# Warming products on written ones, the constants on ScalarE's DMA queue, and u's fourth block copied before the first sines

## The chip, the cores and the metric

One core of one Trainium2 chip runs the whole program. The metric is the device time of one execution in microseconds (us). Of the kernel before, three runs are shown, with their median. A profile of one further execution gives the span that the trace covers.

## What is computed

Two blocks of a model work one after the other on 256 tokens of width 1024, all in float32. The change touches only the first microseconds of the first block:

```python
h = rms_norm(x, norm_w)                  # x: 256 x 1024
proj = h @ w_in                          # u_s is the first 1024 of its columns
# s5_branch(u_s): a complex diagonal recurrence over the 256 tokens,
# per group: ab = exp(lam * dt), bb = f(lam, dt) * b, y = Re(C h) + d * u
...
x = x + m @ w_o
# second block: two gated mixers, then 32 experts, two for each token
hid = silu(xb @ w1[e]) * (xb @ w3[e])
out = out.at[tok].add((hid @ w2[e]) * w)
```

## The kernel before

The program is written by hand for each engine: five instruction streams (SyncE, ScalarE, VectorE, GpSimd, TensorE), joined by semaphores. The order inside each stream is the order of the Python code. Weights stream from memory through the ring, a few slots in one large tile `mem`, each DMA waiting until the products that read its slot are done.

What the start does, by engine:

- SyncE's queue issues the DMAs: the first part of the constants (`con`, 202.5 KB: the unit matrix, ones, the parameters of the recurrence), then x turned (`x_turned`, a view of `xn`) in two halves, between them the weights of u's first two blocks, then the rest of u's weights, `ssm_b`, `ssm_c`, the other constants, and the weight units one after the other.
- TensorE first runs six products of the unit matrix with `con` into bank 7, whose results nobody reads. Then it projects u in eight blocks (`project_u`), of 16 records each in the trace (every product of 256 columns in float32 is two records). Blocks 0 and 1 are made from the input times its gains (`raw`), blocks 2 to 7 from the normed input `hT`. Two PSUM banks are used in turn (`pj`), so block j waits until block j - 2 has been copied out. Between block 0 and block 1 stands the sum of squares, between block 3 and block 4 the inputs of the first two pairs of the scan. The 26 dense projections follow, and before them TensorE waits until blocks 6 and 7 of u are copied out.
- ScalarE squares the input, copies u's blocks 2 to 7 out of PSUM (`take_u`), and makes decay factors, sines and cosines for each of 16 pairs (`trig(pr)`: seven activations and at times a table load). `trig(pr)` waits for the angles of pair pr (`phase_ready`, VectorE's `angle_sums`).
- VectorE multiplies the gains onto x, adds the squares, works out the recurrence's parameters in small instructions (`decay_factors`), scales blocks 0 and 1 of u and makes `hT`. Then come the tables of angles, the angles of pair 0, those of the rotary embedding (`rope_angles`), and for each pair the rotation and two scans.
- GpSimd waits for `ssm_c`, scales it in six instructions of 1024 columns (L589 to L591), and then finishes the states of each pair (L601 to L606).

`banks[7]` is next used by the experts, and `Hr_` by GpSimd's first pair.

Of the kernel before, what the change touches and what calls it, by code (L numbers as in the profile page):

```python
# [48 lines left out]
NCONST1 = CONST_AT["none"][0]  # L49
# [44 lines left out]
def mark(ins, sig):  # L94
    sig.made += 1
    ins.then_inc(sig.sem, 1)
    return sig.made


def link(eng, ins, sig):  # L100

    eng.wait_ge(sig.sem, mark(ins, sig))
# [149 lines left out]
def build(nc, A, out):  # L252
    stack = ExitStack()
    with stack:
        def sb(name, shape, dt=F32):
            return stack.enter_context(nc.sbuf_tensor(name, shape, dt))

        def sem(name):
            return stack.enter_context(nc.semaphore(name))
# [7 lines left out]
        con = sb("con", [P, NCONST])  # L267
        small = sb("small", [P, 972])
        psum = stack.enter_context(nc.psum_tensor("psum", [P, 8, 512], F32))
        banks = [psum[:, i, :] for i in range(8)]  # L270

        def C(name):
            a, w = CONST_AT[name]
            return con[:, a:a + w]

        ident = C("ident")
# [3 lines left out]
        def carve(start, sizes):  # L280

            got, at = [], start
            for n in sizes:
                got.append(area[:, at:at + n])
                at += n
            assert at <= 22528, at
            return got

        def bc(ap, shape):
            return ap.to_broadcast(shape)  # L290
# [9 lines left out]
        def load_unit(sp, n):  # L300
            s = n % SLOTS_BLOCKS
            if n >= SLOTS_BLOCKS:

                pj.to_read(sp, last_fill[FRONT[n - SLOTS_BLOCKS][0]])
            sp.dma_start(ring[:, s, :], A["front"][n]).then_inc(slot_loaded[s], 16)
# [83 lines left out]
        def load_sixth(sp, side):  # L389
# [14 lines left out]
        uT_, BTr_, BTi_, CTr_, CTi_, fa_, fb_, Hr_, Hi_, ptmp2, qT_, kT_, v_ = carve(  # L404
            0, [2048, 1024, 1024, 1024, 1024, 512, 512, 1024, 1024, 512, 3072, 3072, 3072])
# [65 lines left out]
        for name, s in ([(f"u{n}", PJ_U + 4 * n + 3) for n in range(2)]  # L471
# [8 lines left out]
        con_in, con2_in, misc_in, bt_in, ct_in, xre_in = (sem(s) for s in (  # L480
            "con_in", "con2_in", "misc_in", "bt_in", "ct_in", "xre_in"))
# [3 lines left out]
        act1, dve1, pool1 = Signal(sem("act_step1")), Signal(sem("dve_step1")), Signal(sem("pool_step1"))  # L485
# [60 lines left out]
            return range(TP_ATT + 2 * a, TP_ATT + 2 * a + 2)  # L546

        def sync_of_first_layer(sp):
            sp.dma_start(con[:, 0:NCONST1], A["constants"][:, 0:NCONST1]).then_inc(con_in, 16)
            for n in range(2):  # L550
                sp.dma_start(x_turned[:, 4 * n:4 * n + 4, :], A["xT"][:, 4 * n:4 * n + 4, :]).then_inc(xT_in[n], 16)
                sp.dma_start(ring[:, 0, 1024 * n:1024 * n + 1024], A["front"][0, :, 1024 * n:1024 * n + 1024]).then_inc(u_block_in[n], 16)
            sp.dma_start(ring[:, 0, 2048:4096], A["front"][0, :, 2048:4096]).then_inc(slot_loaded[0], 16)
            for n, dst in enumerate((BTr_, BTi_)):
                sp.dma_start(dst, A["ssm_b"][n]).then_inc(bt_in, 16)
            load_unit(sp, 1)
            for n in range(2):
                sp.dma_start(c_raw[n], A["ssm_c"][n]).then_inc(ct_in, 16)
            sp.dma_start(con[:, NCONST1:], A["constants"][:, NCONST1:]).then_inc(con2_in, 16)
            for n in range(2, 2 + len(DENSE) + 2):  # L560
                load_unit(sp, n)

            sp.wait_ge(qk_ready.sem, 6)
            for s in range(2):
                tq.after_read(sp, 10 + s)
            sp.dma_start(xres[:, :, :], A["x"][0].rearrange("(i p) n -> p i n", p=P)).then_inc(xre_in, 16)
            sp.wait_ge(y_free.sem, 8)

            def load(dst, src, **kw):
                sp.dma_start(dst, src, **kw).then_inc(par2_in, 16)  # L570

            for r in range(2):
                load(lb2[:, r], A["hg_lb_2"][r].rearrange("(k p) -> p k", p=P), allow_slow_non_contiguous=True)
            load(hgain, A["hg_out_norm_2"][0].partition_broadcast(P))
            load(dgain[:, 0], A["da_q_norm_2"][0].partition_broadcast(P))
            load(dgain[:, 1], A["da_k_norm_2"][0].partition_broadcast(P))
            load(ogain, A["da_out_norm_2"][0].partition_broadcast(P))
            load(lamv, A["da_lambda_2"][0].partition_broadcast(P))
            for n in range(2 + len(DENSE) + 2, n_units1 + SLOTS_BLOCKS):
                load_unit(sp, n)  # L580
# [31 lines left out]

        def scalar_of_first_layer(act):

            act.dma_start(posi[:, :], A["att_positions"]).then_inc(misc_in, 16)
            act.wait_ge(con_in, 16)
            act.activation(prm[:, DT, :], given[:, DT, :], ACT.Exp).then_inc(dt_ready, 1)
# [13 lines left out]
            def take_u(j):  # L631
                pj.to_read(act, PJ_U + j)
                pj.emptied(act.activation(uT[:, j, :], pj.tile(j)[:, 0:256], ACT.Copy), PJ_U + j)  # L633

            def trig(pr):
                b = pr % 2
                act.wait_ge(phase_ready.sem, pr + 1)
                if pr >= 2:
                    act.wait_ge(state_ready.sem, pr - 1)
                act.activation(decay[:, b, :, 1:256], bc(mag_c[:, 2 * pr:2 * pr + 2].unsqueeze(2), [P, 2, 255]), ACT.Copy)  # L640
                mark(act.activation(sin_t[:, b], phase[:, b], ACT.Abs, bias=quarter_off), act1)
                link(act, act.activation(cos_t[:, b], phase[:, b], ACT.Abs), act1)
                mark(act.activation(sin_t[:, b], sin_t[:, b], ACT.Abs, bias=half_off), act1)
                link(act, act.activation(cos_t[:, b], cos_t[:, b], ACT.Abs, bias=half_off), act1)
                act.activation(sin_t[:, b], sin_t[:, b], ACT.Sin, scale=TURN, bias=halfpi_off)
                link(act, act.activation(cos_t[:, b], cos_t[:, b], ACT.Sin, scale=TURN, bias=halfpi_off), trig_ready)

            take_u(2)
            trig(0)
            for j in range(3, 6):  # L650
                take_u(j)
            trig(1)
            for j in range(6, 8):
# [110 lines left out]
            act.activation(rows2, banks[2][:, 0:256], ACT.Copy).then_inc(rows2_ready, 1)  # L764

        def tensor_of_first_layer(pe):
            pe.wait_ge(con_in, 16)
            for n in range(6):
                pe.matmul(banks[7][:, 0:256], ident, con[:, 0:256], start=True, stop=True)

            def sum_of_squares():
                pe.wait_ge(sq_added, 3)
# [183 lines left out]
            ins.then_inc(xT2_full, 1)  # L956

        def vector_of_first_layer(dve):
            dve.wait_ge(dt_ready, 1)
            R = lambda a: given[:, a, :] if a < DT else prm[:, a, :]  # L960
            mark(dve.tensor_tensor(R(LRDT), R(LR), R(DT), ALU.mult), dve1)
# [203 lines left out]
            for a in range(ATT_STEPS):  # L1165
# [9 lines left out]
                if a in (4, 5):  # L1175
                    n = a - 4
# [566 lines left out]
        @block.sync  # L1743
        def _(sp):
            sync_of_first_layer(sp)
            sp.wait_ge(m_done, 4)
            load_ahead(sp, 3)
# [40 lines left out]
        @block.scalar  # L1788
        def _(act):
            scalar_of_first_layer(act)  # L1790
            for h in range(4):
                pj.after_read(act, PJ_HF + h)
# [87 lines left out]
        @block.tensor  # L1880
        def _(pe):
            tensor_of_first_layer(pe)
            def turn(first, n_fills, blocks):

# [189 lines left out]
        @block.vector  # L2074
        def _(dve):
            vector_of_first_layer(dve)

            dve.wait_ge(rows2_ready, 1)
# [195 lines left out]
```

## Time and profile before

| | |
|---|---|
| three runs | 1087.08, 1085.91, 1088.96 us |
| median | 1087.08 us |
| span of the profiled execution | 1084.6 us |
| TensorE busy, products | 942.7 us |
| DMA, read and written | 292.91 MB |

The three runs are whole executions; the span is what the trace of a fourth one covers, 2.5 us less than the median of the three. For that fourth execution no time other than its span is listed. Times in the rows count from the span's start. A row of the timeline gives start, duration, engine, line, operation and operands, the count of instructions merged into it, and in brackets how long the engine had been idle and what ended that.

### The profile page before, as it was taken

How to read it: one execution, taken by the hardware profiler on the slowest of the kernel's cores; microseconds unless marked ns; L12 is line 12 of the kernel's file. 1: busy time of each engine (PE TensorE's matmuls, PEld its weight loads, DVE VectorE, ACT ScalarE, POOL GpSimd, SP SyncE). 2: the span in 40 equal slices, each digit the busy share in tenths (PEclk: the TensorE clock that was granted, in tenths of full speed). 3: DMA queues.
4: the chain of work that ended last, by engine and by line, in shares of the span. 5: the costliest groups of instructions: out<-in, count | busy, mean ns of one | idle time of the engine just before them, and what ended most of it. 6: DMA issues, size and time to landing. Idle time of an engine off the chain costs nothing.

```text
span 1084.6 us, 12689 instructions
## 1 busy us (share of the span) xinstructions
PE 942.7 (87%) x5090; PEld 555.3 (51%) x5090; DVE 419.4 (39%) x714; ACT 256.1 (24%) x627; POOL 155.4 (14%) x107
## 2 busy tenths in 40 slices
PE   8999999999999999999999998956766666665956
PEld 6655655668888857544788854423221313131412
DVE  7979898835622123253633314221111102020201
ACT  3595978424421012222222020000000000000000
POOL 1776777830000000000000000000000000000000
PEclk9999999999999999999999999998797969798788
DMA  9444243252244446543234699999999999999997
GB/s 366 184 156 149 85 156 136 105 189 88 79 155 155 155 156 257 192 148 134 79 146 154 264 424 387 428 424 426 425 430 424 430 426 430 428 427 428 427 429 318
DMA packets 29121, 292.91 MB, mean 270 GB/s; under 512 B 7568, under 2 KB 8592, under 8 KB 10640
## 3 DMA queue, kind: packets, MB, share of 16 engines
q1 hardware_dynamic: 28928, 292.24, 66.4%
q8 instruction: 33, 0.54, 0.2%
q14 instruction: 16, 0.13, 0.0%
q10 hardware_dynamic: 144, 0.00, 0.0%
HBM read 291.18 MB, written 1.05 MB: 269 GB/s over the span
## 4 chain that ended last, share of the span: by engine, by line
PE 58%; DMA 29%; DVE 5%; issue 3%; ACT 2%; POOL 2%; SPq 0%; DVEq 0%; POOLq 0%; ACTq 0%
DMA mem<-in_experts 29%; PE psum L338 15%; PE psum L345 8%; PE psum L329 7%; PE psum L317 6%; PE psum L322 5%; PE psum L1553 3%; PE psum L1533 2%; PE psum L1570 1%; PE psum L1580 1%; PE psum L1903 1%; PE psum L826 1%; PE psum L890 1%; PE psum L1585 1%; PE psum L878 1%
## 5 line engine op out<-in xcount | busy, mean ns | idle before, releaser
L1553 PE MATMUL psum<-mem 128*32 128x512 f32 x1016 | 144.1, 699 | 82.3 <-DMA mem<-in_experts 82.2
L329 PE MATMUL psum<-mem,hT 128*128 128x512 f32 x288 | 126.3, 595 | 0.5 <-ACT mem L633 0.5
L1553 PEld LDWEIGHTS psum<-mem 128*32 128x32 f32 x1016 | 30.9, 118 | 176.6 <-DMA mem<-in_experts 111.2
L338 PE MATMUL psum<-hT,mem 128*128 128x256 f32 x512 | 115.2, 381 | 0.0
L338 PEld LDWEIGHTS psum<-hT,mem 128*128 128x128 f32 x512 | 95.6, 190 | 15.9 <-issue 2.9
L329 PEld LDWEIGHTS psum<-mem,hT 128*128 128x128 f32 x288 | 55.7, 196 | 64.5 <-issue 63.5
L338 PE MATMUL psum<-mem 128*128 128x256 f32 x320 | 69.7, 379 | 0.0
L317 PE MATMUL psum<-mem,hT 128*128 128x512 f32 x160 | 69.2, 592 | 0.0
L1713 DVE SCALAR_TENSOR_TENSOR mem<-mem,psum 128x512 f32<-128x512 f32 x8 | 5.5, 687 | 155.1 <-ACT mem L1455 155.1
L338 PEld LDWEIGHTS psum<-mem 128*128 128x128 f32 x320 | 60.6, 190 | 8.1
L345 PE MATMUL psum<-hT,mem 128*128 128x256 f32 x256 | 57.6, 382 | 0.0
L1580 PE MATMUL psum<-mem 128*32 128x512 f32 x244 | 42.5, 809 | 16.4 <-DMA mem<-in_experts 12.0
L322 PE MATMUL psum<-mem 128*128 128x512 f32 x128 | 55.6, 592 | 0.0
L1453 ACT ACTIVATE mem<-psum 128x256 f32<-128x256 f32 x8 | 3.1, 383 | 212.4 <-PE psum L1561 212.4
L345 PEld LDWEIGHTS psum<-hT,mem 128*128 128x128 f32 x256 | 48.0, 190 | 7.0
L317 PEld LDWEIGHTS psum<-mem,hT 128*128 128x128 f32 x160 | 30.2, 190 | 36.9 <-issue 36.8
L1083 DVE TENSOR_TENSOR_SCAN mem<-mem 128x512 f32<-128x512 f32 x32 | 46.2, 1482 | 0.0
L1570 PE MATMUL psum<-mem 128*128 128x256 f32 (+1 forms) x96 | 36.6, 505 | 7.2 <-DVE mem L1718 7.2
L1722 DVE TENSOR_TENSOR xn<-xn,psum 128x256 f32<-128x256 f32 (+1 forms) x42 | 21.4, 510 | 53.5 <-PE psum L1570 53.3
L322 PEld LDWEIGHTS psum<-mem 128*128 128x128 f32 x128 | 24.2, 190 | 28.8 <-issue 28.7
L1533 PE MATMUL psum<-mem,xres 128*128 128x128 f32 x256 | 32.5, 288 | 7.0 <-issue 6.3
L1533 PEld LDWEIGHTS psum<-mem,xres 128*128 128x128 f32 x256 | 31.9, 204 | 8.6 <-issue 7.6
(368 smaller groups left out, 1208.2 us busy)
## 6 DMA issues: line engine op xcount, KB each, us to landing
mem<-in_experts SPq DMA_DIRECT2D x87, 2048.0 KB, 35.6
mem<-in_front SPq DMA_DIRECT2D x39, 2048.0 KB, 7.8
mem<-in_experts SPq DMA_DIRECT2D x15, 1024.0 KB, 34.4
con<-in_constants SPq DMA_DIRECT2D x1, 1035.0 KB, 18.2
xn<-in_xT SPq DMA_DIRECT2D x2, 512.0 KB, 5.4
mem<-in_front SPq DMA_DIRECT2D x2, 512.0 KB, 7.3
mem<-in_front SPq DMA_DIRECT2D x1, 1024.0 KB, 10.0
mem<-in_ssm_b SPq DMA_DIRECT2D x2, 512.0 KB, 11.1
```

What stands on the lines that cost most here:

```text
L317: ins = pe.matmul(dst, lhs[:, k, P * i:P * i + P], w[:, k, c0:c0 + 512], start=(k == 0), stop=(k == nk - 1))
L322: ins = pe.matmul(dst, lhs[:, k, P * i:P * i + P], w[:, k, c0:c0 + 512], start=(k == 0), stop=(k == lhs.shape[1] - 1))
L329: ins = pe.matmul(dst, tokens[:, k, i], w[:, k, :], start=(k == 0), stop=(k == KD - 1))
L338: ins = pe.matmul(dst[:, at:at + T], w[:, k, P * m:P * m + P], rhs[:, k, :], start=(k == 0), stop=(k == nk - 1))
L345: ins = pe.matmul(dst, w[:, k, P * m:P * m + P], rhs[:, k, :], start=(k == 0), stop=(k == nk - 1))
L826: ins = pe.matmul(banks[4 + 2 * (a % 2) + w][:, at:at + keys.stop - keys.start], qT[r, g, j, P * i:P * i + P], kT[r, g, j, keys], start=Tr ...
L1083: ins = dve.tensor_tensor_scan(out=dst[:, b], data0=decay_[:, 512 * b:512 * b + 512], data1=src, initial=0.0, op0=ALU.mult, op1=ALU.add)
L1533: ins = pe.matmul(bank[:, P * (k % 4):P * (k % 4) + P], xres[:, i, P * k:P * k + P], selx_[:, P * i:P * i + P], start=(i == 0), stop=(i == 1))
L1553: ins = pe.matmul(banks[m // 2 % 2][32 * q:32 * q + 32, :], xgT[:, k, 32 * q:32 * q + 32], w[q][:, FF * kk:FF * kk + FF], start=(k == 0), ...
L1570: pe.matmul(total(n), selT_[:, P * i:P * i + P], y_[:, at:at + width], start=True, stop=True).then_inc(combined, 1)
L1580: ins = pe.matmul(banks[2][r, :], hidT[:, k, r], w[q][:, 512 * kk:512 * kk + 512], start=(k == 0), stop=(k == 3), tile_position=(0, 32 * q))
L1722: dve.tensor_tensor(dst, x if isinstance(it, int) and it == 0 else dst, total(n), ALU.add).then_inc(added, 1)
```

## The change

Four edits. The constants' first DMA goes from SyncE's queue to the head of ScalarE's. TensorE's first products are five instead of six, on a stretch of `Hr_` that VectorE fills with 1.0 as its first instruction, and they wait for that instead of for the constants, for which TensorE now waits behind them. ScalarE copies u's block 3 before `trig(0)` instead of behind it.

```diff
         def sync_of_first_layer(sp):
-            sp.dma_start(con[:, 0:NCONST1], A["constants"][:, 0:NCONST1]).then_inc(con_in, 16)
             for n in range(2):
...
         def scalar_of_first_layer(act):
 
+            act.dma_start(con[:, 0:NCONST1], A["constants"][:, 0:NCONST1]).then_inc(con_in, 16)
             act.dma_start(posi[:, :], A["att_positions"]).then_inc(misc_in, 16)
             act.wait_ge(con_in, 16)
...
             take_u(2)
+            take_u(3)
             trig(0)
-            for j in range(3, 6):
+            for j in range(4, 6):
                 take_u(j)
             trig(1)
...
         def tensor_of_first_layer(pe):
+            pe.wait_ge(dve1.sem, 1)
+            for n in range(5):
+                pe.matmul(banks[7][:, 0:256], Hr_[:, 0:128], Hr_[:, 0:256], start=True, stop=True)
             pe.wait_ge(con_in, 16)
-            for n in range(6):
-                pe.matmul(banks[7][:, 0:256], ident, con[:, 0:256], start=True, stop=True)
...
         def vector_of_first_layer(dve):
+            mark(dve.memset(Hr_[:, 0:256], 1.0), dve1)
             dve.wait_ge(dt_ready, 1)
```

On ScalarE, from the activation of the norm (L629) to the start of pair 1's `trig`; L633 is `take_u`, L640 to L646 are one `trig`. Before:

```order
L629 ACTIVATE mem<-psum,con 128x256
L633 ACTIVATE mem<-psum 128x256
L640 ACTIVATE mem<-small 128x2x255
L641 ACTIVATE mem<-mem,con 128x512
L642 ACTIVATE mem<-mem 128x512
L643 ACTIVATE mem<-mem,con 128x512
L644 ACTIVATE mem<-mem,con 128x512
L645 ACT_TABLE_LOAD
L645 ACTIVATE mem<-mem,con 128x512
L646 ACTIVATE mem<-mem,con 128x512
L633 ACTIVATE mem<-psum 128x256 x3
L640 ACTIVATE mem<-small 128x2x255
```

And of the change, the same place:

```order
L629 ACTIVATE mem<-psum,con 128x256
L633 ACTIVATE mem<-psum 128x256 x2
L640 ACTIVATE mem<-small 128x2x255
L641 ACTIVATE mem<-mem,con 128x512
L642 ACTIVATE mem<-mem 128x512
L643 ACTIVATE mem<-mem,con 128x512
L644 ACTIVATE mem<-mem,con 128x512
L645 ACT_TABLE_LOAD
L645 ACTIVATE mem<-mem,con 128x512
L646 ACTIVATE mem<-mem,con 128x512
L633 ACTIVATE mem<-psum 128x256 x2
L640 ACTIVATE mem<-small 128x2x255
```

One copy has moved from behind pair 0's `trig` to before it; the copies of blocks 4 and 5 are still behind pair 0's, those of 6 and 7 behind pair 1's.

On SyncE's queue, the head of the program (xn is x turned, in_front the weights of u). Before:

```order
L549 DMA con<-in_constants 128x405
L551 DMA xn<-in_xT 128x1024
L552 DMA mem<-in_front 128x1024
L551 DMA xn<-in_xT 128x1024
L552 DMA mem<-in_front 128x1024
L553 DMA mem<-in_front 128x2048
L555 DMA mem<-in_ssm_b 128x1024 x2
L305 DMA mem<-in_front 128x4096
L558 DMA mem<-in_ssm_c 128x1024 x2
```

And of the change:

```order
L550 DMA xn<-in_xT 128x1024
L551 DMA mem<-in_front 128x1024
L550 DMA xn<-in_xT 128x1024
L551 DMA mem<-in_front 128x1024
L552 DMA mem<-in_front 128x2048
L554 DMA mem<-in_ssm_b 128x1024 x2
L305 DMA mem<-in_front 128x4096
L557 DMA mem<-in_ssm_c 128x1024 x2
```

Each DMA behind the constants has moved up by one place on SyncE's queue.

On TensorE, the first rows with their waits. Before:

```order
L769 MATMUL psum<-con 128x256 [waits con_in]
L769 MATMUL psum<-con 128x256 x5
L790 MATMUL psum<-xres,mem 128x256 [waits raw_ready,u_block0_in]
L790 MATMUL psum<-xres,mem 128x256 [waits raw_ready] x7
L774 MATMUL psum<-mem,con 128x256 [waits sq_added]
```

And of the change:

```order
L770 MATMUL psum<-mem 128x256 [waits dve_step1]
L770 MATMUL psum<-mem 128x256 x4
L792 MATMUL psum<-xres,mem 128x256 [waits raw_ready,u_block0_in,con_in]
L792 MATMUL psum<-xres,mem 128x256 [waits raw_ready] x7
L776 MATMUL psum<-mem,con 128x256 [waits sq_added]
```

The first product no longer waits for the constants, and block 0 of u does as well as for what it waited for.

## Rows read from the trace of the kernel before

**Rows 1.** Busy time of each engine, from the page.

```profile
PE 942.7 (87%) x5090; PEld 555.3 (51%) x5090; DVE 419.4 (39%) x714; ACT 256.1 (24%) x627; POOL 155.4 (14%) x107
```

**Rows 2.** Stages at the end: busy of PE, PEld, DVE, ACT, POOL; PEclk, DMA share, GB/s.

```profile
700.00:1085.00 385.00, 258.54 (x1830) 92.66 (x1822) 51.26 (x93) 15.65 (x35) 0.00 (x0) 0.84 0.99 419
```

**Rows 3.** The chain that ended last, 100 to 120 us.

```profile
101.16 2.14 POOL mem L606
...
112.08 0.68 ACT mem L710
```

**Rows 4.** TensorE's timeline, 43 to 320 us.

```profile
112.89 0.63 PE L865 MATMUL psum<-con,xres 128*128 128x128 f32 x4 [1.00 <-ACT mem L710]
```

**Rows 5.** GpSimd's and VectorE's timelines, 20 to 60 us.

```profile
23.19 2.27 POOL L589 TENSOR_TENSOR mem<-mem 128x1024 f32<-128x1024 f32 x1 [22.74 <-DMA mem<-in_ssm_c]
...
34.16 2.37 POOL L591 TENSOR_TENSOR mem<-mem 128x1024 f32<-128x1024 f32 x1
...
23.86 2.15 DVE L1053 TENSOR_TENSOR mem<-mem 128x512 f32<-128x512 f32 x1
...
34.35 2.66 DVE L1040 SCALAR_TENSOR_TENSOR small<-small 128x16 f32<-128x16 f32 x3
...
37.13 0.69 DVE L1053 TENSOR_TENSOR mem<-mem 128x512 f32<-128x512 f32 x1
37.73 0.68 DVE L1067 TENSOR_TENSOR mem<-mem,psum 128x512 f32<-128x512 f32 x1
```

**Rows 6.** All engines' timeline, 0 to 22 us.

```profile
0.74 0.40 SPq L549 DMA_DIRECT2D con<-in_constants  x1
...
1.19 0.42 SPq L551 DMA_DIRECT2D xn<-in_xT  x1
...
3.37 4.81 PE L769 MATMUL psum<-con 128*128 128x256 f32 x12 [3.37 <-DMA con<-in_constants]
...
8.20 3.72 PE L790 MATMUL psum<-xres,mem 128*128 128x256 f32 x16
...
9.41 1.14 DVE L989 TENSOR_SCALAR xres<-xn,con 128x256 f32<-128x256 f32 x4 [1.88 <-DMA xn<-in_xT]
...
15.82 1.74 DVE L1000 RECIPROCAL mem<-mem 128x256 f32<-128x256 f32 x1
```

**Rows 7.** Stages of the start, in the columns of rows 2.

```profile
1.50:2.50 1.00, 0.00 (x0) 0.00 (x0) 0.00 (x0) 0.97 (x1) 0.00 (x0) 1.00 0.64 122
...
4.00:6.50 2.50, 2.50 (x7) 1.95 (x6) 2.33 (x7) 1.97 (x5) 0.00 (x0) 1.00 0.82 220
...
12.00:32.00 20.00, 16.46 (x84) 13.39 (x84) 19.11 (x39) 6.80 (x12) 8.65 (x4) 1.00 1.02 428
```

**Rows 8.** The warming products by their line: ns min/median/max.

```profile
L769 PE MATMUL psum<-con x12: 379/631/792, 3.4 to 7.8; 128*128 128x256 f32 x12
```

**Rows 9.** TensorE's timeline, 17 to 45 us.

```profile
18.50 7.14 PE L790 MATMUL psum<-hT,mem 128*128 128x256 f32 x32 [1.37 <-DVE hT L1009]
...
26.65 3.72 PE L790 MATMUL psum<-hT,mem 128*128 128x256 f32 x16
32.38 10.60 PE L790 MATMUL psum<-hT,mem 128*128 128x256 f32 x48 [2.01 <-ACT mem L633]
43.50 1.96 PE L329 MATMUL psum<-mem,hT 128*128 128x512 f32 x4 [0.52 <-ACT mem L633]
```

**Rows 10.** ScalarE's timeline, 15 to 45 us.

```profile
26.04 0.63 ACT L640 ACTIVATE mem<-small 128x510 f32<-128x510 f32 x1 [3.44 <-DVE mem L1053]
...
31.85 0.66 ACT L633 ACTIVATE mem<-psum 128x256 f32<-128x256 f32 x2
36.10 0.38 ACT L633 ACTIVATE mem<-psum 128x256 f32<-128x256 f32 x1 [3.60 <-PE psum L790]
37.85 0.63 ACT L640 ACTIVATE mem<-small 128x510 f32<-128x510 f32 x1 [1.36 <-DVE mem L1053]
...
42.38 0.38 ACT L633 ACTIVATE mem<-psum 128x256 f32<-128x256 f32 x1
43.01 0.38 ACT L633 ACTIVATE mem<-psum 128x256 f32<-128x256 f32 x1 [0.25 <-PE psum L790]
```

## The prediction

> **What bounds the kernel now.** I read the page first: TensorE is busy for 942.7 us, 87% of the span [rows 1]. That share hides two regimes. In the last 385 us the DMA engines are busy for a share of 0.99 at 419 GB/s [rows 2], so the end waits for the experts' weights; those DMAs wait for ring slots that TensorE frees, so what TensorE gains or loses before about 600 us should move the end by as much. The question is what bounds TensorE in the first 113 us, where all four edits act.
>
> The chain that ended last answers it. At 112.08 us it is in a ScalarE copy (L710), before that in ScalarE's `trig`, and before that in GpSimd's L606 at 101.16 [rows 3]. TensorE's own timeline agrees: at 112.89 us it has been idle for 1.00 us, until that copy [rows 4], and from 43.50 to there it shows no idle time. So TensorE reaches 112 us with 1.00 us in hand, and time that it gains before only makes this wait longer. What counts is the chain through VectorE, GpSimd and ScalarE.
>
> I followed that chain back. VectorE's rotation of pair 0 (L1067) starts at 37.73, directly behind the angles of pair 1 (L1053, 37.13) [rows 5]. Ahead of that stand tiny instructions that take far longer than their size. The three L1040, on 16 columns, take 2.66 us together, and an L1053 at 23.86 takes 2.15 us where the one at 37.13 takes 0.69. All of it lies beside GpSimd's six products on `ssm_c`, from 23.19 to 34.16 + 2.37 = 36.53 us [rows 5]. The reader is to see that VectorE gets free only when GpSimd's last one ends, and that GpSimd's start is set by a landing: it waited 22.74 us for `ssm_c`. So the start of the path is the arrival of `ssm_c`, not the arrival of x, nor TensorE.
>
> Before 23 us VectorE is a chain of its own: it waits 1.88 us for the second half of x, starts on it at 9.41, and comes to the reciprocal at 15.82 [rows 6]; TensorE waits for it at 18.50. But its slack against GpSimd's hold begins at 23.86 - 23.19 = 0.67 us: up to that much earlier, its L1053 still falls into GpSimd's first product and ends with it.
>
> **Edit 1, the constants on the other queue.** SyncE's queue issues the constants at 0.74 and x's first half at 1.19 [rows 6], so each later DMA is issued 0.45 us earlier, `ssm_b`, the first whole unit and `ssm_c` among them. The bytes ahead of `ssm_c` stay the same, and from 12 to 32 us the engines are at a share of 1.02 [rows 7]: an earlier issue into a full pipe lands nothing earlier. What can be gained is the unused part at the start. From 1.50 to 2.50 the share is 0.64, so 1 x 0.36 = 0.36 us of all engines' time is free. From 4.00 to 6.50 it is 0.82 at only 220 GB/s, when more DMAs have been issued than can be in work, so issue isn't what is missing there [rows 7]. The bounds for `ssm_c` are 0 (all lost to the interleaving of two queues) and 0.45 us (the whole issue). I take 0.3, near the 0.36 that the row shows as free. For x's second half the same 0.3 holds; it is below 0.67, so it hides under GpSimd's hold. The Trainium skill, DMA: Bandwidth & Descriptors, section Issuing engines are not separate DMA queues, speaks against this edit: DMAs started by different engines run on the same 16 DMA engines and interleave, and only the sequencer's issue time is saved. By that rule the sum would be between the two bounds too, nearer to 0.
>
> The constants themselves may land later, as they now share the engines with x's first half. What waits for them is ScalarE's first exponential and VectorE's small chain, which comes to x's second half 1.88 us early [rows 6]: 1.88 us of cover, cost 0. ScalarE issues one more DMA, some 0.4 us by L549's row, before its first table load; the cover is the same. The position DMA, behind it, is read by VectorE only after 25 us. Cost 0.
>
> **Edit 2, the warming products.** They began at 3.37, when the constants landed, and took 4.81 us for 12 records, 0.40 us each; the next 16 took 3.72 us, 0.23 each [rows 6]. By duration they are 631 ns in the median and 379 at least [rows 8]: they ran at the lower of the two levels (1.2 GHz), and block 0 of u at the upper (2.4 GHz), though the clock column says 1.00 throughout. Now 10 records start behind a fill of 256 columns, at about 1.3 us (my estimate from the first activity at 1.19 us on ScalarE), and end at about 1.3 + 10 x 0.40 = 5.3. Then TensorE waits until the first weights of u, about 8.2 - 0.3 = 7.9 us. Whether block 0 then runs at the upper level is not to be read from any row. It decides little: all 16 records of block 0 at 0.40 us give 7.9 + 6.4 = 14.3, the sum of squares 4 x 0.40 later 15.9, and the norm on ScalarE some 0.5 us later, at 16.4, against VectorE's reciprocal at 15.82 [rows 6]. That is 0.6 us later at worst, within the slack that ends at GpSimd's second product at 25.4. I take 0. VectorE's fill of about 0.3 us lies in the time when it waits for the constants. Cost 0.
>
> **Edit 3, u's block 3 copied before the sines.** TensorE ends block 3 at 18.50 + 7.14 = 25.64, block 4 at 30.37, and then waits 2.01 us, till 32.38, for the copy of block 3, which stands behind `trig(0)` and comes at 31.85 [rows 9, 10]. Now the copy runs from about 25.7 to 26.1, the wait of 2.01 us goes, and `trig(0)`, behind it on ScalarE, starts at 26.1 instead of 26.04. Behind `trig(0)` VectorE waits at 37.73, and `trig(0)` ends at 31.85: 5.9 us of cover. So blocks 5 to 7 end 2.0 us earlier, at about 32.38 + 10.60 - 2.01 = 41.0. But what is late next? TensorE may go on only when blocks 6 and 7 are copied, and those copies stand behind `trig(1)`, which starts at 37.85 because it waited 1.36 us for VectorE's angles, and whose last sine is followed by the copies from 42.38 on [rows 10]. Both together take 0.66 us as the pair at 31.85 did, so TensorE starts at 42.38 + 0.66 + 0.11 = 43.15, where the 0.11 is the distance from the last copy's end (43.39) to 43.50 before. Of 2.01 us only 0.35 are left, and a wait of about 2.1 us stands at 41 us. And these 0.35 us come to 112.89, where TensorE waits anyway. The term is 0, with the bounds 0 and 2.0 (the wait gone for good).
>
> **The sum.** The chain at 37.13 moves with `ssm_c`: -0.3. Edits 2 and 3: 0. The span goes from 1084.6 to 1084.3. The runs' median stands 2.5 us above the span, so the time is 1087.08 - 0.3 = 1086.8 us.
>
> **Rivals.**
> 1. *Edit 1 does nothing*: the two queues interleave, `ssm_c` lands as before; 1087.1. For it: the full pipe from 12 us on [rows 7]. Against: the free 0.36 us.
> 2. *The 2.0 us of edit 3 reach the end*, with the 0.3: 1084.8. This needs VectorE's angles of pair 1, and so `trig(1)`, 2 us earlier too, and the chain at 112 us with them. Against it stands that nothing of edit 3 touches VectorE before 37 us, and the 1.00 us of idle [rows 4].
> 3. *Slower, by a cold TensorE behind the moved copy*: edit 3 puts `trig(0)` behind block 3. If TensorE falls back while it waits from 5.3 to 7.9 and stays at 0.40 us a record, block 1 ends at 15.9 + 6.4 = 22.3, blocks 2 and 3 at 22.3 + 32 x 0.40 = 35.1, and `trig(0)` runs from 35.5 to 41.3 where VectorE wanted it at 37.73: +3.6 us, 1090.7. It decides from the point where block 3 ends later than 25.6 + 5.9 = 31.5 us. Against: before, the lower level lasted some 4 us of products [rows 6], so it should be over by about 12 us. The Trainium skill, TensorE: Matmul & The Clock Gate, Part 1, says the throttled state is the default and comes back after idle time; the idle time of 2.01 us at 32.38 was followed by records of 10.60 / 48 = 0.22 us [rows 9].
> 4. *Relief from GpSimd's hold*: the relative place of both engines shifts so that VectorE's rotary angles slip past. Then pair 0 could start when `trig(0)` ends, 37.73 - 31.85 = 5.9 us earlier: 1081.2. It needs a shift of several us, and the edits give tenths.
> 5. *x's second half lands later*, as its first half shares with the constants. Within 1.5 us it hides in GpSimd's second product (23.86 to 25.4); I put +1.0: 1088.1.
>
> **How the numbers follow.** The forecast 0.48, rival 1 0.20, rival 2 0.13, rival 3 0.07, rival 4 0.05, rival 5 0.07. The predicted time is the forecast's, 1086.8. The range takes in rivals 1, 2 and 5 and the spread of the three runs (1.5 us to each side of the forecast would be 1085.3 to 1088.3), and leaves out 3 and 4: 1084.3 to 1088.8. Only rivals 3 and 4 pass the 0.3%, or 3.3 us, that a measurement of this kernel can tell from no change: slower 0.07, faster 0.07 (rival 4 and the edge of rival 2), same 0.86.
>
> **What would show it.** In the profile after: `ssm_c`'s wait on GpSimd ends at 22.9 (22.7 to 23.2); no wait of TensorE near 32, but one of about 2.1 us that ends at 43.2, on L633; the wait at 112.9 grown to about 1.1; 10 warming records from 1.3 us on. The prediction is wrong if TensorE goes on before 42.5 us, if the copy at 112.08 moves by more than 1 us, or if block 3 ends after 31 us. It would be wrong in its frame if the end did not follow the chain at 112 us, because the weights' stream at the end starts from something else.

## The result

| | before | changed |
|---|---|---|
| median of five runs | 1087.08 us | 1092.36 us |
| lowest to highest | 1085.91 to 1088.96 | 1087.90 to 1093.89 |
| ratio, 95% interval | | 1.0040 [1.0025, 1.0055] |
| span of the profiled execution | 1084.6 us | 1086.1 us |

The change is slower, by 0.4%; I had forecast 1086.8, with 1088.8 as the upper end. A ratio, here and below, is the measured one that its interval belongs to, and not the quotient of the two medians, which differ here by 5.3 us. The profile fell on the fastest of the five executions, so its 1.5 us in the span are less than the usual cost of some 5 us; a second profile of the same kernel, below, has a span of 1089.8. Line numbers of VectorE's code are higher by 3 in the changed kernel, GpSimd's lower by 1.

Its timeline from 0 to 22 us answers to [rows 6]:

```profile
0.74 0.41 ACTq L614 DMA_DIRECT2D con<-in_constants  x1
...
1.20 4.63 PE L770 MATMUL psum<-mem 128*128 128x256 f32 x10 [1.20 <-DVE mem L961]
...
5.44 0.23 ACT L617 ACTIVATE mem<-con 128x32 f32<-128x32 f32 x1 [2.48 <-DMA con<-in_constants]
...
8.48 2.19 DVE L992 TENSOR_SCALAR xres<-xn,con 128x256 f32<-128x256 f32 x8
...
8.98 5.38 PE L792 MATMUL psum<-xres,mem 128*128 128x256 f32 x16 [3.15 <-DVE xres L992]
...
15.94 1.74 DVE L1003 RECIPROCAL mem<-mem 128x256 f32<-128x256 f32 x1
```

The constants land 4.7 us after their issue instead of 2.6 (ScalarE reads them at 5.44; TensorE read them at 3.37 before). VectorE therefore starts on x at 8.48, when both halves are there, and is done with all eight instructions at 10.67 against 9.41 + 1.14 = 10.55 before. It comes to the reciprocal 0.12 us later, nearly even.

The timelines of GpSimd and VectorE, 20 to 60 us (VectorE to 115), answer to [rows 5]:

```profile
22.27 2.13 POOL L588 TENSOR_TENSOR mem<-mem 128x1024 f32<-128x1024 f32 x1 [21.82 <-DMA mem<-in_ssm_c]
...
22.67 2.02 DVE L1029 TENSOR_SCALAR mem<-mem 128x512 f32<-128x512 f32 x1
24.72 2.28 DVE L1030 TENSOR_TENSOR mem<-mem 128x512 f32<-128x512 f32 x1
...
27.16 2.59 DVE L1056 TENSOR_TENSOR mem<-mem 128x512 f32<-128x512 f32 x1
...
37.03 0.69 DVE L1056 TENSOR_TENSOR mem<-mem 128x512 f32<-128x512 f32 x1
...
60.60 0.69 DVE L1070 TENSOR_TENSOR mem<-mem,psum 128x512 f32<-128x512 f32 x1 [7.66 <-PE psum L802]
```

GpSimd starts 0.92 us earlier (22.27 against 23.19), and two more of VectorE's instructions, L1029 and L1030, run beside it and take 2.02 and 2.28 us. In the kernel before, they are L1026 and L1027, and the second started just ahead of GpSimd's 23.19 and took its own time:

```profile
23.00 0.69 DVE L1027 TENSOR_TENSOR mem<-mem 128x512 f32<-128x512 f32 x1
```

They stand ahead of the angles of pair 0, which now end at 29.75 instead of 26.01. The angles of pair 1 are not late (37.03 against 37.13). But `trig(0)` is, and behind it stand the copies of blocks 4 and 5 (ScalarE's timeline, to compare with [rows 10], and then TensorE's, with [rows 9] and [rows 4]):

```profile
29.79 0.63 ACT L640 ACTIVATE mem<-small 128x510 f32<-128x510 f32 x1 [3.60 <-DVE mem L1056]
...
35.60 0.66 ACT L633 ACTIVATE mem<-psum 128x256 f32<-128x256 f32 x2
```

```profile
26.77 7.17 PE L792 MATMUL psum<-hT,mem 128*128 128x256 f32 x32
36.12 8.83 PE L792 MATMUL psum<-hT,mem 128*128 128x256 f32 x32 [2.18 <-ACT mem L633]
45.48 13.98 PE L329 MATMUL psum<-mem,hT 128*128 128x512 f32 x32 [0.52 <-issue]
...
114.33 0.63 PE L867 MATMUL psum<-con,xres 128*128 128x128 f32 x4 [0.45 <-ACT mem L711]
```

TensorE no longer waits for the copy of block 3, but 2.18 us for that of block 4, and starts the dense projections at 45.48 instead of 43.50. The 32 records behind the wait take 8.83 us, where 0.22 us each would give 7.1. The stage view of 36 to 40 us (columns as in [rows 2]) says why: the granted clock, third from the end, is 0.57, between the two levels over the stage. So of the 1.98 us by which the projections are late, some 1.7 (8.83 - 7.1) are the lower clock behind the wait, and the late copies alone leave some 0.3.

```profile
36.00:40.00 4.00, 3.88 (x10) 3.18 (x11) 3.83 (x11) 2.47 (x5) 0.10 (x1) 0.57 0.00 0
```

From 45.48 on the delay is carried: at 60.60 VectorE has waited 7.66 us for TensorE's products of the scan's inputs, and at the place of [rows 4] TensorE is 114.33 - 112.89 = 1.44 us late. That is the 1.98 us of 45.48 less the 0.55 us by which its wait there shrank (1.00 to 0.45). The span grew by 1.5. The wait doesn't shrink to nothing, because the ScalarE copy that ends it has itself become late: the chain that ended last now runs through TensorE's products. Two rows of that chain, and one of ScalarE's timeline:

```profile
36.12 8.83 PE psum L792 x32
...
45.48 7.13 PE psum L329 x16
```

```profile
52.69 0.60 ACT L694 ACTIVATE xres<-psum 128x512 f32<-128x512 f32 x1 [6.76 <-PE psum L329]
```

ScalarE's copy at 52.69 waits for the first of TensorE's projections, and ScalarE's next sines stand behind that copy.

### The profile page after: what moved, and what is told of

Same layout as the page of the kernel before. It is cut to its first block, busy times and chain, and to the rows that moved or that the text cites. A ratio compares the mean times of both kernels' runs of the same rounds, so it can differ in the third digit from the quotient of the medians.

```text
span 1086.1 us, 12686 instructions
## 1 busy us (share of the span) xinstructions
PE 944.3 (87%) x5088; PEld 556.7 (51%) x5088; DVE 420.1 (39%) x715; ACT 256.0 (24%) x627; POOL 156.5 (14%) x107
## 4 chain that ended last, share of the span: by engine, by line
PE 57%; DMA 33%; DVE 4%; ACT 3%; issue 2%; POOL 1%; SPq 0%; DVEq 0%; ACTq 0%; POOLq 0%
DMA mem<-in_experts 32%; PE psum L338 15%; PE psum L345 8%; PE psum L329 8%; PE psum L317 6%; PE psum L322 5%; PE psum L1556 3%; PE psum L1906 1%; PE psum L1583 1%; PE psum L1573 1%; PE psum L792 1%; PE psum L828 1%; PE psum L892 1%; PE psum L880 1%; PE psum L1536 1%
## 5 line engine op out<-in xcount | busy, mean ns | idle before, releaser
L329 PE MATMUL psum<-mem,hT 128*128 128x512 f32 x288 | 126.3, 595 | 0.5 <-issue 0.5
L329 PEld LDWEIGHTS psum<-mem,hT 128*128 128x128 f32 x288 | 55.7, 196 | 64.5 <-issue 64.4
```

The source lines that it names most:

```text
L329: ins = pe.matmul(dst, tokens[:, k, i], w[:, k, :], start=(k == 0), stop=(k == KD - 1))
```

## The experiments

Four theories. An instruction is called held where it lasts as long as the GpSimd product beside it. **H**: the cost is the meeting of VectorE and GpSimd: whatever brings GpSimd's six products earlier, or VectorE's instructions later, adds held instructions ahead of the first sines. **C**: it is TensorE's clock, by the early warming products. **L**: it is the late landing of the constants or the DMA order as such. **W**: it is edit 3, the copy of block 3 ahead of the sines. Times are medians in us, ratios to the kernel before, which was run again with each group.

### One edit at a time, and two

```diff
# edit 1 alone, in the streams of SyncE and ScalarE
-            sp.dma_start(con[:, 0:NCONST1], A["constants"][:, 0:NCONST1]).then_inc(con_in, 16)
+            act.dma_start(con[:, 0:NCONST1], A["constants"][:, 0:NCONST1]).then_inc(con_in, 16)
# edit 2 alone
-                pe.matmul(banks[7][:, 0:256], ident, con[:, 0:256], start=True, stop=True)
+                pe.matmul(banks[7][:, 0:256], Hr_[:, 0:128], Hr_[:, 0:256], start=True, stop=True)
+            mark(dve.memset(Hr_[:, 0:256], 1.0), dve1)
# edit 3 alone
             take_u(2)
+            take_u(3)
             trig(0)
```

Edit 1 alone. 

> Edit 1 alone: the constants on ScalarE's queue, all else as before. Theory H (GpSimd's hold): the cost comes from ssm_c landing 0.9 us earlier, so that GpSimd's first products catch two more of VectorE's instructions; then this run shows the angles of pair 0 ending at about 29.8 us as in the change (26.0 before), and is slower than before by 2 to 5 us. Theory C (TensorE's clock, from the early warming products): edit 2 is missing here, block 0 of u runs at the upper level, and the time is within 1 us of before. Theory W (the copy of block 3 ahead of the sines): no change, as edit 3 is missing.

Edit 2 alone. 

> Edit 2 alone: five warming products on written ones, the constants first on SyncE's queue as before. Theory C: TensorE idles from about 5.5 to 8.2 us and block 0 of u runs at the lower level in some executions; slower by 1 to 5 us, and a wider spread than the 3 us of before. Theory H: within 0.5 us of before, since no DMA moved. Theory W: no change.

Edit 3 alone. 

> Edit 3 alone: u's block 3 copied ahead of the first sines. My recorded working: TensorE's wait of 2.0 us at 32 us goes, one of about 2.1 us comes at 41 us, the time is within 0.5 us of before. Theory W: slower by 2 us or more. Theories H and C: no change.

Edits 2 and 3. 

> Edits 2 and 3, that is the change with the constants back on SyncE's queue. Theory H: the slowdown is gone, within 1 us of before, angles of pair 0 end near 26 us. Theory C: slower by as much as the change, 4 to 5 us in the median.

| | median | ratio, interval |
|---|---|---|
| before, in this group | 1087.23 | |
| edit 1 | 1092.21 | 1.0051 [1.0031, 1.0071] |
| edit 2 | 1087.39 | 1.0004 [0.9995, 1.0013] |
| edit 3 | 1087.79 | 1.0005 [0.9996, 1.0015] |
| edits 2 and 3 | 1087.03 | 1.0003 [0.9994, 1.0012] |

Edit 1 alone costs as much as all edits together; C and W fall as the main cause, as far as medians go. VectorE's timeline with edit 1 alone:

```profile
22.34 2.37 DVE L1025 TENSOR_TENSOR mem<-small,con 128x512 f32<-128x512 f32 x1
24.75 2.02 DVE L1026 TENSOR_SCALAR mem<-mem 128x512 f32<-128x512 f32 x1
26.80 2.72 DVE L1027 TENSOR_TENSOR mem<-mem 128x512 f32<-128x512 f32 x1
...
29.69 2.15 DVE L1053 TENSOR_TENSOR mem<-mem 128x512 f32<-128x512 f32 x1
```

Three instructions are held here, not two, since this VectorE comes another 0.4 us later. Its reciprocal, which waits for the norm, starts at 16.34 instead of 15.82: the warming products stand behind the late constants (5.74 instead of 3.37), and block 0 and the sum of squares behind them. So in this run the late constants have a part in the meeting, from VectorE's side. On TensorE's timeline of the same run the copies behind `trig(0)` come so late that it waits 7.31 us:

```profile
38.21 12.63 PE L790 MATMUL psum<-hT,mem 128*128 128x256 f32 x48 [7.31 <-ACT mem L633]
51.35 8.83 PE L329 MATMUL psum<-mem,hT 128*128 128x512 f32 x20 [0.52 <-issue]
```

Edit 2 alone has a median like that of before, but its 12 runs go from 1085.96 to 1089.94, and three are above the highest of the 29 runs of before beside them (1088.83). Its profile fell on an execution of 1089.53 and shows the meeting without edit 1. TensorE, GpSimd, VectorE and TensorE again:

```profile
8.23 6.73 PE L791 MATMUL psum<-xres,mem 128*128 128x256 f32 x16 [3.17 <-DMA mem<-in_front]
...
23.45 1.91 POOL L589 TENSOR_TENSOR mem<-mem 128x1024 f32<-128x1024 f32 x1 [23.00 <-DMA mem<-in_ssm_c]
...
23.56 2.34 DVE L1029 TENSOR_TENSOR mem<-mem 128x512 f32<-128x512 f32 x1
...
34.59 11.64 PE L791 MATMUL psum<-hT,mem 128*128 128x256 f32 x45 [3.66 <-ACT mem L633]
```

Block 0 takes 6.73 us instead of 3.72, at a granted clock of 0.50 from 8 to 14 us. The norm comes later by that, and L1029 (L1027 of before) starts at 23.56 instead of 23.00, now 0.11 us behind GpSimd instead of 0.19 us ahead of it, and is held. TensorE's wait is 3.66 us. So edit 2 can cross the same edge by itself, where under H I had expected at most 0.5 us; the wider spread that C foretold is there, by way of H's meeting. In how many executions the edge is crossed, one profile doesn't show.

Edit 3 alone shows my recorded working nearly to the digit, and one thing that it missed. TensorE's timeline and the stage from 43 to 50 us:

```profile
26.84 14.08 PE L791 MATMUL psum<-hT,mem 128*128 128x256 f32 x64
43.29 3.55 PE L329 MATMUL psum<-mem,hT 128*128 128x512 f32 x4 [2.37 <-ACT mem L633]
```

```profile
43.00:50.00 7.00, 6.71 (x12) 3.04 (x13) 6.97 (x10) 0.71 (x4) 5.87 (x4) 0.76 0.62 260
```

The wait near 32 us is gone, one of 2.37 us ends at 43.29 (forecast: 2.1 and 43.15). Behind it the granted clock is 0.76, where the kernel before has 1.00 in the same stage: the first four records take 3.55 us against 1.96 in [rows 9]. So the 0.2 us of gain at 43 us turns into a loss, 0.96 us at the place of [rows 4] in this profile (113.85), and no gain is left.

### The meeting itself

```diff
# gate_before (gate in q_gate, gate_copy, gate_all, gate_warm_copy too)
   pool.wait_ge(prm_ready, 1)
+  pool.wait_ge(rope_in, 1)        # the rotary angles are done
# vector_late: the kernel before, after scale_rows()
+  link(dve, dve.memset(Hr_[:, 0:512], 0.0), dve1)
```

Edit 1 with the wait. 

> Edit 1 alone, and GpSimd's products on ssm_c wait for the rotary angles (rope_in), so that none of VectorE's small instructions runs beside them. Theory H (the cost of edit 1 is that VectorE falls into GpSimd's hold): the cost is gone; the angles of pair 0 end near 25 us, time below before, 1083 to 1086 us. Rival theory L (the cost is the later landing of the constants, 5.4 to 5.7 us instead of 3.35): the wait on GpSimd changes nothing of that, 1091 to 1093 us as edit 1 alone.

The kernel before with the wait. 

> The kernel before with the same wait on GpSimd and nothing else. Theory H: the angles of pair 0 end at 24.5 instead of 26.0, pair 0's rotation can start when its sines end (about 30.4 instead of 37.7 us); the copies before TensorE's wait at 32 us come 1.5 us earlier, and the chain at 113 us gets shorter until TensorE bounds it: 1083.5 to 1086 us. Theory L says nothing against it; a third view, that the place of GpSimd's products doesn't matter, says 1087.

Edit 3 with the wait. 

> The kernel before with the wait on GpSimd and edit 3 (block 3 copied ahead of the first sines). With the hold gone, trig(1) is no longer late, so that the 2 us of edit 3 should now get through: TensorE starts its dense projections near 41 us instead of 43.5. Theory H: 1082.5 to 1085 us, below the wait alone. If the copies still stand behind trig(1), it equals the wait alone.

VectorE half a microsecond later. 

> The kernel before with one fill of 512 columns (about 0.5 us, its result is read by nobody) put on VectorE behind the scaling of u, and nothing else: VectorE comes 0.5 us later to GpSimd's first product, the DMAs are untouched. Theory H: one instruction more (L1027) is held, the angles of pair 0 end near 28 us instead of 26, and the time rises by 0.5 to 3 us. If the cost came from DMA order alone (theory L), it is within 0.5 us of before.

| | median | ratio, interval |
|---|---|---|
| before, in this group | 1087.09 | |
| q_gate | 1085.46 | 0.9982 [0.9974, 0.9991] |
| gate_before | 1084.09 | 0.9967 [0.9955, 0.9980] |
| gate_copy | 1084.97 | 0.9977 [0.9968, 0.9985] |
| vector_late | 1091.25 | 1.0035 [1.0022, 1.0047] |

`vector_late` is the cleanest of all: no DMA's issue has moved, and 0.5 us of work on VectorE costs 1091.25 - 1087.09 = 4.2 us. VectorE's and TensorE's timelines of it:

```profile
21.34 0.48 DVE L1021 MEMSET mem<- 128x512 f32 x1
...
23.92 2.28 DVE L1028 TENSOR_TENSOR mem<-mem 128x512 f32<-128x512 f32 x1
```

```profile
34.88 11.42 PE L790 MATMUL psum<-hT,mem 128*128 128x256 f32 x44 [4.27 <-ACT mem L633]
```

One instruction more is held (2.28 us), and TensorE's wait at 32 us grows to 4.27, by 2.26 us. Behind it all 48 records of blocks 5 to 7 (the view holds 44 of them) take 12.29 us instead of 10.60: another 1.7 us, at a granted clock of 0.62 from 36 to 40 us. I had put 3 us as the most, and had the held instruction in it but not the clock behind the longer wait. The other way round, the wait on GpSimd takes away edit 1's cost (1092.2 to 1085.5, below the kernel before) although the constants still land at 5.7 us: L falls as a cause by itself. With the wait VectorE's instructions have their own length, here in `gate_before`, with the second place of interest below it:

```profile
24.00 0.69 DVE L1054 TENSOR_TENSOR mem<-mem 128x512 f32<-128x512 f32 x1
...
25.76 0.59 DVE L1041 SCALAR_TENSOR_TENSOR small<-small 128x16 f32<-128x16 f32 x3
...
31.80 0.69 DVE L1071 TENSOR_TENSOR psum<-mem,psum 128x512 f32<-128x512 f32 x1
...
34.19 4.89 DVE L1084 TENSOR_TENSOR_SCAN mem<-mem 128x512 f32<-128x512 f32 x2
```

```profile
31.05 10.60 PE L791 MATMUL psum<-hT,mem 128*128 128x256 f32 x48 [0.55 <-ACT mem L634]
42.17 4.11 PE L329 MATMUL psum<-mem,hT 128*128 128x512 f32 x9 [0.52 <-issue]
```

TensorE waits 0.55 us instead of 2.01 and starts at 42.17 instead of 43.50. `gate_copy` starts earlier still, near 41.1 us as expected, but its median is not below that of the wait alone. At the place of [rows 4] its profile is only 0.59 us ahead of `gate_before` (110.43 and 111.02), with a wait of 0.90 instead of 0.44, so nearly half of the 1.0 us ends in that wait. The intervals overlap, and I can't say more than that edit 3 shows no gain here either. `gate_before` has the lowest median of the study, from five runs.

### The changed kernel again, ssm_c later, and the wait on all of it

```diff
# c_later: the changed kernel, on SyncE's queue
+            sp.dma_start(con[:, NCONST1:], A["constants"][:, NCONST1:]).then_inc(con2_in, 16)
             for n in range(2):
                 sp.dma_start(c_raw[n], A["ssm_c"][n]).then_inc(ct_in, 16)
-            sp.dma_start(con[:, NCONST1:], A["constants"][:, NCONST1:]).then_inc(con2_in, 16)
```

The changed kernel once more. 

> The changed kernel once more, for a second profile, since the first one fell on the fastest of its five executions (1087.9 us against 1091.3 to 1093.9). Theory H: the time follows the number of VectorE's instructions that GpSimd holds ahead of the first sines (two in the first profile, L1029 and L1030, besides L1056); in a profile near 1092 us there are three, the angles of pair 0 end near 32 us, and TensorE waits over 5 us for the copies of blocks 4 and 5. If the profile near 1092 shows the same two, the spread has another cause.

ssm_c later. 

> The changed kernel with ssm_c issued behind the second part of the constants (1 MB, about 2.4 us of the stream, later), all else the same. Theory H in its form that the early landing of ssm_c decides: GpSimd starts near 24.7 us, the angles of pair 0 pass ahead of it, and most of the cost is gone: 1086 to 1089 us (GpSimd ends later and holds the rotary angles till about 39 us). In its form that the late constants decide, or theory L: 1091 to 1093 as the change.

The changed kernel with the wait. 

> The changed kernel with the wait on GpSimd. Theory H: below the kernel before, 1083.5 to 1086 us, and no faster than the wait alone (1084.1), since the three edits carry at most tenths once the hold is gone.

Edits 2 and 3 with the wait. 

> Edits 2 and 3 and the wait on GpSimd, the constants on SyncE's queue as before. Between the wait alone (1084.1) and the wait with edit 3 (1085.0): 1083.5 to 1085.5 us. If early warming products cost something, it is at the upper end and above gate_all.

| | median | ratio, interval |
|---|---|---|
| before, in this group | 1086.49 | |
| after_again | 1091.90 | 1.0043 [1.0026, 1.0059] |
| c_later | 1084.82 | 0.9992 [0.9979, 1.0005] |
| gate_all | 1084.99 | 0.9982 [0.9973, 0.9991] |
| gate_warm_copy | 1085.16 | 0.9983 [0.9974, 0.9992] |

The second profile of the changed kernel, on VectorE and on TensorE:

```profile
16.53 1.75 DVE L1003 RECIPROCAL mem<-mem 128x256 f32<-128x256 f32 x1 [0.47 <-ACT mem L629]
...
22.32 1.78 DVE L1027 COPY small<-mem 128x32 f32<-128x32 f32 x1
24.13 2.35 DVE L1028 TENSOR_TENSOR mem<-small,con 128x512 f32<-128x512 f32 x1
26.51 2.46 DVE L1029 TENSOR_SCALAR mem<-mem 128x512 f32<-128x512 f32 x1
29.00 2.28 DVE L1030 TENSOR_TENSOR mem<-mem 128x512 f32<-128x512 f32 x1
```

```profile
39.97 9.44 PE L792 MATMUL psum<-hT,mem 128*128 128x256 f32 x32 [5.43 <-ACT mem L633]
```

Four instructions are held where the first profile had two (I expected three), the wait is 5.43 us, and the span is 1089.8. The same kernel thus has times some us apart by where its two engines meet. The first row shows why VectorE came later this time: it waited 0.47 us for the norm, which block 0 delays, with 6.10 us for its 16 records where the first profile had 5.38. Edit 2 so has a part in how many are held.

`c_later` keeps the late constants and both other edits, and only lets GpSimd start at 25.44. The angles of pair 0 run ahead of it (25.05, 0.69 us), and in the median the cost is gone. But its twelve runs fall into two groups, seven from 1083.3 to 1084.9 and five from 1088.2 to 1089.5, and the profile is of one of the five (1089.08). In it nothing is held ahead of the first sines. What it has is edit 3's wait, with the lower clock behind it, and a VectorE that waited 0.74 us for the norm:

```profile
44.30 7.95 PE L329 MATMUL psum<-mem,hT 128*128 128x512 f32 x14 [2.38 <-ACT mem L633]
```

The first 32 records of L329, of which the view holds 14, take 15.68 us where the kernel before had 13.98. What the seven shorter executions look like no profile shows. With `vector_late` and `q_gate` this says that the cost of the change is the early start of GpSimd against VectorE, and not the constants' landing as such. The four kernels with further edits and the wait have ratios of 0.9977 to 0.9983, not better than the wait alone (0.9967); their intervals overlap with its interval.

## Why the prediction was wrong

- **The frame held in the main.** What TensorE is late by at the place of [rows 4] is about what the end is late by: 1.44 there and 1.5 in the span; in `vector_late` 3.65 and 3.2; in `gate_before` 111.02 - 112.89 = -1.87 and -1.6. It is not exact: `q_gate` is 1.64 us early there (111.25), and its span is 0.1 us longer than before.
- **The step that failed is edit 1's**, in "The chain at 37.13 moves with `ssm_c`: -0.3", and in the sentence on the slack of 0.67 us. I read GpSimd's hold as a fixed block into which VectorE's L1053 falls, and asked only how much earlier VectorE may come. The other side I did not ask: what is next in line to be caught. L1027 started at 23.00, 0.19 us ahead of GpSimd's 23.19 ([rows 5]), and `ssm_c` came 0.92 us earlier, not 0.3, and outside my bounds of 0 to 0.45. My forecast moved both engines earlier by the same 0.3, which keeps the 0.19. But my worst case of edit 2 brought VectorE 0.6 us later, three times the distance to the edge, and I called that free. In the changed kernel VectorE comes 0.12 us later and GpSimd 0.92 earlier, and two instructions are caught. Rival 5 made the same mistake from the other end, when it let VectorE come 1.5 us later at a price of 1.0: `vector_late` shows 4.2 us for 0.5.
- **The second half of that step** was the path. I followed the chain that ended last, on which only the angles of pair 1 stand, and these moved by 0.10 us (37.03), not by 0.3 and not with `ssm_c`: GpSimd's last product ends 0.70 us earlier (33.48 + 2.35 = 35.83), but VectorE, with two more instructions held before, still has small ones to do. But the angles of pair 0 lead by `trig(0)` and the copies to TensorE, and a delay of 3.7 us there is not covered. I had computed 5.9 us of cover for `trig(0)` against VectorE, and none against the copies behind it. Nor did TensorE have the 1.00 us in hand that I read at 112.89. In the profiles slower than before that wait is still 0.43 to 0.46, so that 0.55 us was its slack, and what it gets late by beyond that reaches the end.
- **The clock** behind a longer wait was no term of the sum. It is 1.7 of the 1.98 us in the first profile and 1.7 us in `vector_late`.
- **The constants' landing** was as foreseen in kind: 1.88 us of cover for a delay of 2.1, and 0.12 us later at the reciprocal.
- **Edit 2** was sized rightly as to the median (1.0004), and wrongly as to its slack: block 0 did run in part or wholly at the lower level (5.38 us for 16 records in the first profile, 6.10 in the second, 6.73 with edit 2 alone), and the time by which the norm was then late counted, because later means more held.
- **Edit 3** was right in place and size (wait of 2.37 at 43.29), except for the clock behind the new wait, 0.76.
- **Of the rivals**, none has this mechanism. Rival 3 has the right place (`trig(0)` late) with the wrong cause for it, at 1090.7; the lower clock that it feared came only behind the later wait. Rival 4 asked for a shift of several us to get free of the hold; the wait on GpSimd does that and gives 3.0 us, half of the 5.9 computed. VectorE's rotation of pair 0 starts 7.1 us earlier there (30.59), but the chain then runs through TensorE.

What stays open: why taking one DMA off SyncE's queue brings the issue of `ssm_c` forward by more than the 0.45 us that I had as the upper bound. Its two issues begin 0.58 us and end 1.04 us earlier (the kernel before, then the changed one):

```profile
5.96 1.45 SPq L558 DMA_DIRECT2D mem<-in_ssm_c  x2
```

```profile
5.38 0.99 SPq L557 DMA_DIRECT2D mem<-in_ssm_c  x2
```

So my sentence that issue isn't what is missing from 4.00 to 6.50 us does not hold as it stands: the issuing itself took longer before. Nor does a run show how an earlier issue, into a pipe that I took as full, lands 0.92 us earlier, or why the constants take 4.7 us beside x's first half. Why a wait of 2.18 us is followed by the lower clock and one of 2.01 us is not stays open too.

## What to carry to other kernels

Where two engines hold each other up, look for the edge on both sides: which instruction is last to get out before the other engine starts, and by how much. Here 0.19 us stood between the kernel and 4 us, and a reordering of DMAs far ahead, half a microsecond of work or a slower block of products could each cross that edge; make such a meeting explicit with a wait instead of leaving it to a landing. And follow not only the chain that ended last but each queue behind a delayed instruction, with the slack of whoever waits for it.

## What the runs showed of the hardware

An instruction of VectorE that reads and writes SBUF lasts, beside GpSimd's products, about as long as GpSimd's one, whatever its size: a copy of 32 columns took 1.78 us, and two scans took 4.89 us in `gate_before` against 2.33 in the changed kernel while GpSimd was idle. Those that read from PSUM are not held: L1071 took 0.69 us in `gate_before` with GpSimd busy beside it. Nor is a fill, which reads nothing: L1111 of the changed kernel took 0.06 us at 27.07, inside GpSimd's product from 26.53 to 29.21.

The Trainium skill, Advanced Engine Details and Errata, VectorE Performance Modes, says that the second SBUF port of VectorE is shared with GpSimd and that its 2-port instructions and GpSimd's block each other, with source and destination in SBUF as a condition of those. The held copy agrees with that. But the section's table has no 2-port mode for an addition or product of two tensors, and those (TENSOR_TENSOR with both inputs in SBUF, 2.15 to 2.72 us instead of 0.69) are held here just the same.

Edit 3 alone, `q_only`, `vector_late` and the changed kernel each show TensorE's granted clock below 1.00 behind a wait of 2.2 to 7.3 us (0.76 in the stage from 43 to 50 us, 0.71 from 40 to 44, 0.62 and 0.57 from 36 to 40), but the kernel before had a wait of 2.01 us at 32 us and stayed at 1.00. A wait that has been harmless need not be so when it moves by a few us or grows by tenths.
